# Seventeen of thirty modulation column blocks, weighted on VectorE and GpSimd and summed over rows by one matmul each, in place of eight matmul steps each

## The reference, cut to what matters

```python
silu_c = jax.nn.silu(c)            # (1, 1024), latents
silu_cc = jax.nn.silu(c_ctx)       # (1024,),  context
for l in range(DEPTH):             # DEPTH = 2
    m_lat = (silu_c @ w_mod[l] + b_mod[l]).reshape(Bsz, N_MOD, 1, D)    # N_MOD = 9
    m_ctx = (silu_cc @ w_mod[l] + b_mod[l]).reshape(N_MOD, D)
    x = x + 0.5 * m_lat[:, 2] * swiglu(modulate(rms_norm(x), m_lat[:, 0], m_lat[:, 1]), ...)
    ... mixer with m[3], m[4], m[5]; second feed-forward with m[6], m[7], m[8] ...
```

## Time and profile before

| | |
|---|---|
| runs | 3808.41 us median (3801.29 to 3816.84) |
| profiled execution, first to last instruction | 3809.4 us |
| TensorE busy | 3587.4 us, 94% |
| VectorE busy | 1836.3 us, 48% |
| ScalarE busy | 1418.9 us, 37% |
| GpSimd busy | 60.0 us, 2% |
| modulation matmuls | 960 records (two to a matmul, four matmuls to a step), 143.1 us |

### The profile page before, as it was taken

How to read it: one execution, slowest core, us unless ns; L and a number is a source line. 1 busy time by engine, 2 the same in 40 slices (tenths; PEclk the granted TensorE clock), 3 DMA queues, 4 the chain that set the end, 5 groups by cost and what they waited for, 6 DMA issues and landing times.

```text
span 3809.4 us, 62156 instructions
## 1 busy us (share of the span) xinstructions
PE 3587.4 (94%) x27294; PEld 2960.9 (78%) x27294; DVE 1836.3 (48%) x3143; ACT 1418.9 (37%) x2303; POOL 60.0 (2%) x98
## 2 busy tenths in 40 slices
PE   6999999888889999999987999999999989999898
PEld 4777885677668888877874998777887768879898
DVE  2223445666654233423265553654464443566575
ACT  3123334434334222323244543443243332445553
POOL 0000000000010000000000000020000000010000
PEclk8999999999999999999998999999999999999999
DMA  5454123222243233243225552121324552223463
GB/s 194 163 183 134 59 83 127 102 102 102 102 77 110 91 99 100 90 142 122 89 89 212 174 180 96 58 78 56 100 83 172 177 173 93 89 91 127 145 190 113
DMA packets 257918, 453.93 MB, mean 119 GB/s; under 512 B 14096, under 2 KB 157584, under 8 KB 243184
## 3 DMA queue, kind: packets, MB, share of 16 engines
q1 hardware_dynamic: 253840, 441.68, 34.6%
q0 software_dynamic: 3808, 8.27, 1.3%
HBM read 447.24 MB, written 1.94 MB: 118 GB/s over the span
## 4 chain that ended last, share of the span: by engine, by line
PE 81%; DVE 10%; ACT 4%; DMA 3%; issue 1%; SPq 0%; DVEq 0%; ACTq 0%
PE bank L1072 80%; DVE W L1859 2%; DVE W L1868 2%; DVE WR L1859 2%; DMA ring<-in_w_mod 1%; ACT WR L1524 1%; ACT W L1524 1%; PE bank L1295 1%; DMA ring<-in_w_up 1%; DVE H L1859 1%; DVE HL L1859 1%; DMA ring<-in_w_ada 1%; DVE X L1868 0%; ACT H L1524 0%; DVE small L2136 0%
## 5 line engine op out<-in xcount | busy, mean ns | idle before, releaser
L1072 PE MATMUL bank<-HH,WR 128*128 128x512 f32 (+1 forms) x9312 | 2430.9, 347 | 74.9 <-DVE WR L1859 42.0
L1072 PEld LDWEIGHTS bank<-HH,WR 128*128 128x128 f32 x9312 | 1643.3, 192 | 334.3 <-DVE WR L1859 54.4
L1072 PE MATMUL bank<-HL,WR 128*128 128x512 f32 (+1 forms) x4656 | 1601.3, 344 | 0.0
L1859 DVE TENSOR_TENSOR WR<-ring,WR 128x2048 fp32r<-128x2048 f32 (+3 forms) x300 | 673.8, 2250 | 859.9 <-ACT WR L1524 859.4
L1524 ACT ACTIVATE WR<-ring 128x2048 fp32r<-128x2048 f32 (+3 forms) x300 | 562.6, 1881 | 1200.1 <-PE bank L1072 819.5
L1072 PEld LDWEIGHTS bank<-HL,WR 128*128 128x128 f32 x4656 | 895.4, 192 | 96.9
L1524 ACT ACTIVATE W<-bank 64x256 f32<-64x256 f32 (+4 forms) x662 | 285.8, 442 | 388.6 <-PE bank L1072 342.1
L1072 PE MATMUL bank<-W 64*64 64x64 f32 (+5 forms) x6304 | 351.7, 247 | 41.4 <-ACT W L1524 20.5
L1072 PEld LDWEIGHTS bank<-W 64*64 64x64 f32 (+3 forms) x6304 | 266.1, 140 | 131.6 <-issue 47.2
L1868 DVE SCALAR_TENSOR_TENSOR W<-bank,vec,W 128x510 f32<-128x510 f32 (+1 forms) x206 | 130.6, 634 | 190.2 <-ACT W L1524 186.6
L1524 ACT ACTIVATE W<-bank,small 128x512 f32<-128x512 f32 (+2 forms) x183 | 113.1, 622 | 225.8 <-DVE small L2136 154.1
(11 more groups left out here) (111 smaller groups left out, 2022.0 us busy)
## 6 DMA issues: line engine op xcount, KB each, us to landing
ring<-in_ffn_in SPq DMA_DIRECT2D x176, 512.0 KB, 5.0
ring<-in_w_mod SPq DMA_DIRECT2D x72, 1024.0 KB, 5.4
ring<-in_w_in SPq DMA_DIRECT2D x52, 1024.0 KB, 5.1
ring<-in_w_ada SPq DMA_DIRECT2D x48, 1024.0 KB, 6.5
ring<-in_ffn_out SPq DMA_DIRECT2D x176, 256.0 KB, 3.6
ring<-in_w_up SPq DMA_DIRECT2D x88, 512.0 KB, 5.0
ring<-in_w_down SPq DMA_DIRECT2D x88, 256.0 KB, 3.6
ring<-in_even_w_in SPq DMA_DIRECT2D x8, 1024.0 KB, 5.1
```

Source lines behind the costliest of these rows:

```text
L1072: return e.matmul(o, l, r, start=start, stop=stop, skip_group_check=True)
L1859: put(e.tensor_tensor(o, a, b, op), *events)
```

## The change

Seventeen of the thirty blocks leave `mod_mm`: blocks 2 to 8 of `w_mod[0]`, 0 to 5 of `w_mod[1]`, 0 to 3 of `w_ada[0]`. For each, eight pieces of 128 rows by 1024 columns are loaded. VectorE multiplies a piece by the latents' value of each row and adds it to an accumulator; GpSimd does the same for the context in two instructions (product in place, then sum), except for one block of `w_mod[1]` that the context doesn't need. One TensorE step with ones then sums over the 128 rows (`rows_sum`), and four small matmuls turn the sums into columns (`rows_tr`), one such pair to a block.

All pieces stand in f00, 2 and f10: 40 behind the steps of the first product (a rate of 0.55 pieces to a step; in f10 8 of VectorE alone and 24 of both) and 8 behind the first steps of the second (rate 0.9). One ring slot is set aside for them in these stages, cut in two halves; weights have the other two. A piece's load is issued on GpSimd's queue when the piece two before it has been used by both engines. The silu of both vectors is made once at the start. The scan keeps 12 steps, the second attention 8.

```diff
+        ACC = [[wv(25088, [1024]), wv(27136, [1024])], [wv(9216, [1024]), wv(10240, [1024])]]
...
+        def row_sums(jobs, buf):
+            tail, ahead = [], []
+            for t, idx, nv in jobs:
+                for k in range(KD):
+                    s = rows_slab(TABLES[t][0], k, idx, nv)
+                    ORDER.append(("rows_in", s))
+                    ahead.append(("rows", t, idx, k, s, nv, buf))
+                    if len(ahead) > 1:
+                        ORDER.append(ahead.pop(0))
+                    if tail and k in (2, 4):
+                        ORDER.append(tail.pop(0))
+                    yield
+                now(ahead)
+                tail = [("rows_sum", t, idx, s, nv, buf), ("rows_tr", t, idx, nv)]
+                buf = 1 - buf
+            PENDING.extend(tail)
...
-        cols = {t: columns(t) for t in TABLES}
+        cols = {"m0": columns("m0", [0]), "m1": columns("m1", [3, 4]), "a0": columns("a0", [2]), "a1": columns("a1", [0, 1, 2])}
...
-        ffn("f00", A["ffn_in"][0, 0], A["ffn_out"][0, 0], 0, NT, 0, "ne", (itertools.islice(cols["m0"], 18), 0.85))
+        ffn("f00", A["ffn_in"][0, 0], A["ffn_out"][0, 0], 0, NT, 0, "ne",
+            rows=(row_sums(pairs_of("m0", 2, 7), 0), 0.55, row_sums(pairs_of("m0", 7, 8), 0), 0.9))
...
+            rows=(row_sums(pairs_of("m0", 8, 9) + pairs_of("m1", 0, 4), 0), 0.55, row_sums(pairs_of("m1", 4, 5), 0), 0.9))
-        ffn("f10", A["ffn_in"][1, 0], A["ffn_out"][1, 0], 0, NT, 1, "no", (itertools.islice(cols["a0"], 9), 0.5))
+        ffn("f10", A["ffn_in"][1, 0], A["ffn_out"][1, 0], 0, NT, 1, "no",
+            rows=(row_sums(pairs_of("m1", 5, 6, 1) + pairs_of("a0", 0, 3), 1), 0.55, row_sums(pairs_of("a0", 3, 4), 0), 0.9))
...
-                    if any(use[r] >= i for r in befores(todo[0], "raw")):
+                    if any(use[r] >= i for r in befores(todo[0], "raw", "rows")):
...
             def rows_sum(t, idx, s, nv, buf):                      # TensorE
+                q.wait_ge(DVES, ("rows", s))
+                if nv == 2:
+                    q.wait_ge(POOLS, ("rows", s))
+                for j in range(2):
+                    for v in range(nv):
+                        i = 32 * (nv * j + v)
+                        x = mm(o[i:i + 32, :], C("ones", 0, 32), ACC[buf][v][:, 512 * j:512 * j + 512], True, True)
...
+            def rows(t, idx, k, s, nv, buf):                       # VectorE
+                q.wait_ge(ROWS[SLABS[s]["half"]], ("raw", s))
+                c = SILU[src][:, k:k + 1]
+                if k == 0:
+                    ts(ACC[buf][0], rows_of(s), c, None, ALU.mult, None, ("rows", t, idx, k, 0), ("rows", s))
+                else:
+                    stt(ACC[buf][0], rows_of(s), c, ACC[buf][0], ALU.mult, ALU.add, ("rows", t, idx, k, 0), ("rows", s))
...
+            def rows_in(s):                                        # GpSimd
+                    q.wait_ge(POOLS, ("rows", x["before"])) if SLABS[x["before"]]["nv"] == 2 else q.wait_ge(DVES, ("rows", x["before"]))
+                e.dma_start(rows_of(s), x["parts"][0]).then_inc(ROWS[x["half"]].sem, ROWS[x["half"]].mark(("raw", s), by=16))
+            def rows(t, idx, k, s, nv, buf):                       # GpSimd
+                q.wait_ge(ROWS[SLABS[s]["half"]], ("raw", s))
+                q.wait_ge(DVES, ("rows", s))
+                if k == 0:
+                    e.tensor_scalar(ACC[buf][1], rows_of(s), c, None, ALU.mult).then_inc(...)
+                else:
+                    e.tensor_scalar(rows_of(s), rows_of(s), c, None, ALU.mult).then_inc(...)
+                    q.wait_ge(POOLS, ("rows_product", s))
+                    e.tensor_tensor(ACC[buf][1], ACC[buf][1], rows_of(s), ALU.add).then_inc(...)
```

More of the change, by code:

```diff
@@ L241, in program @@
         SLABS = []
-        hold = {"split": 0, "slots": 3, "slot": -1, "keep": None}
+        hold = {"split": 0, "slots": 3, "slot": -1, "keep": None, "halves": None}
         IN_SLOT = [None] * NS
@@ L268, in slab, with rows_begin, rows_end, rows_slab @@
             return IN_SLOT[i]
+        def rows_begin():
+            i = hold["keep"] = (hold["slot"] + 1) % NS
+            hold["halves"] = [IN_SLOT[i], IN_SLOT[i]]
+        def rows_end():
+            hold["slot"], hold["keep"], hold["halves"] = hold["keep"], None, None
+        def rows_slab(w, k, idx, nv):
+            i, h = hold["keep"], k % 2
+            SLABS.append(dict(parts=[w[P * k:P * k + P, 1024 * idx:1024 * idx + 1024]], kc=1, w=1024, kind="rows", half=h, nv=nv,
+                              split_from=hold["split"], slots=hold["slots"], ring=i, before=hold["halves"][h],
+                              n=sum(x["kind"] == "split" for x in SLABS)))
+            IN_SLOT[i] = hold["halves"][h] = len(SLABS) - 1
+            return IN_SLOT[i]
         def slot(s):
             return ring[SLABS[s]["ring"]]
+        def rows_of(s):
+            h = SLABS[s]["half"]
+            return slot(s).rearrange("p k c -> p (k c)")[:, 1024 * h:1024 * h + 1024]
         def landed(s):
@@ L314, in lin @@
                                     square(kw["norm"], 4 * g + m, h)
+                        if each:
+                            each()
                     if between:
@@ L1014, in program @@
                 use[step[6]] = i
+            if step[0] == "rows":
+                use[step[4]] = i
             if step[0] == "lora_done":
                 use[LORA["s"]] = i
-        befores = lambda s, kind: [x["before"] for x in SLABS[:s + 1] if x["before"] is not None and SLABS[x["before"]]["kind"] == kind]
+        befores = lambda s, *kinds: [x["before"] for x in SLABS[:s + 1] if x["before"] is not None and SLABS[x["before"]]["kind"] in kinds]
         steps, at_hold, behind_ = [], 0, []
         for i, step in enumerate(ORDER):
-            if step[0] in ("slab", "slab_h", "slab_k", "mod_mm"):
+            if step[0] in ("slab", "slab_h", "slab_k", "mod_mm", "rows"):
                 steps += [("rest", s) for s in behind_]
@@ L1026, in program @@
                 assert not todo or todo[0] not in befores(step[6], "split")
+            if step[0] == "rows":
+                assert not todo or todo[0] not in befores(step[4], "split")
             n = None
@@ L1057, in take @@
                 at[0] += 1
-                n = next(i for i, (t, b) in enumerate(shut_) if not (holder[b] and holder[b][0] == "bcast" and at[0] - t < 6))
+                n = next(i for i, (t, b) in enumerate(shut_) if not (holder[b] and holder[b][0] == "bcast" and at[0] - t < 8))
                 b = shut_.pop(n)[1]
@@ L1193, in mod_tr, with rows_sum, rows_tr @@
                            C("sel", 0, 2 * nb, 0, 32 * nb), True, True)
+                x.then_inc(MM.sem, MM.mark(key))
+                shut(key)
+            def rows_sum(t, idx, s, nv, buf):
+                key = ("rows", t, idx)
+                o = take(key)
+                q.wait_ge(IN["first"], ("in", "first"))
+                q.wait_ge(DVES, ("rows", s))
[5 more added lines that the diff above has]
+                        x = mm(o[i:i + 32, :], C("ones", 0, 32), ACC[buf][v][:, 512 * j:512 * j + 512], True, True)
+                x.then_inc(MM.sem, MM.mark(key))
+                shut(key)
+            def rows_tr(t, idx, nv):
+                key = ("rowsc", t, idx)
+                n = 2 * nv
+                q.wait_ge(ACTS, ("mrow", t, "rows", idx))
+                o = take(key)
+                for m in range(4):
+                    x = mm(o[:, n * m:n * m + n], RROW[0:32 * n, m * P:(m + 1) * P], C("sel", 0, 2 * n, 0, 32 * n)[:, ::2], True, True)
                 x.then_inc(MM.sem, MM.mark(key))
@@ L1512, in fourier_b @@
                 shut(("f2", l, n))
-            do = dict(slab=slab_, slab_h=slab_h, slab_k=slab_k, mod_mm=mod_mm, mod_tr=mod_tr, sum=sum_, rstd=rstd, spread=spread, spread_read=spread_read, bar=bar, rope=rope,
+            do = dict(slab=slab_, slab_h=slab_h, slab_k=slab_k, mod_mm=mod_mm, mod_tr=mod_tr, rows_sum=rows_sum, rows_tr=rows_tr, sum=sum_, rstd=rstd, spread=spread, spread_read=spread_read, bar=bar, rope=rope,
                       head_sum=head_sum, head_spread=head_spread, att=att, lora_w=lora_w, lora_a=lora_a, wkv=lambda d: next(streams[d]),
@@ L1535, in silu_c @@
                 src = TABLES[t][3]
[L1536 removed]
+                q.wait_ge(ACTS, ("silu", src))
                 q.wait_ge(DVES, ("silc_zero",))
@@ L2367, in nc_parts @@
                 tt(NCl[:, h, 0:nq], NCO[:, h, 0:nq], Sh[:, h, 0:nq].bitcast(F32), ALU.subtract, ("hl", f"sc{l}", h))
-            do = dict(begin=begin, inputs=inputs, inputs_rest=inputs_rest, rest=rest, mod_tr=mod_tr, rstd=rstd, times=times, mod_l=mod_l,
+            do = dict(begin=begin, inputs=inputs, inputs_rest=inputs_rest, rest=rest, mod_tr=mod_tr, rows=rows, rows_tr=rows_tr, rstd=rstd, times=times, mod_l=mod_l,
```

123 lines of the change are left out of this document (103 added, 20 removed).

## The result

| | before | after |
|---|---|---|
| runs, median | 3812.62 us (3801.29 to 3818.58, 4 runs) | 4047.41 us (4040.88 to 4057.56, 4 runs) |
| ratio | | 1.0623, 95% interval 1.0601 to 1.0645 |
| profiled span | 3809.4 us | 4046.5 us |
| mean granted clock | 0.974 | 0.946 |

Slower, as forecast, but by 235 us in the medians (237 between the two profiled executions) and not by 46: outside the range of 3778 to 3925. The rival nearest to it was the third (GpSimd is slow, 4002 us, given 0.09).

What follows compares the result with a forecast made beforehand. TensorE, with 81% of the chain of waits, was taken as the bound. Terms 7 - 48 + 47 (first products) + 32 + 8 = +46 on the profiled 3809.4 us gave 3855, 1 less against the median: 3854 us; range 3778 to 3925.

Steps and rivals of the forecast that it cites:

- the third rival: Feed-forwards: GpSimd slow, a piece every 6.4 us against 5.0 due even without exclusion; +194 us, 4002 us; chance 0.09.
- Elsewhere, forecast -48: Modulation steps leaving the scan (-24), first attention (-12, range -6 to -18) and second attention (-12): together -48 us.
- Own TensorE work, forecast +7: Feed-forwards: seventeen `rows_sum` and `rows_tr` add 36.0 us, the departing modulation work takes away 28.8: +7 us.
- GpSimd's pair, taken at 3.13 us: GpSimd's product and sum on a piece: three operand reads at ScalarE's 1.043 us, 3.13 us; ends 1.97 and 6.3.
- The forecast's own formula: Time per piece under exclusion: VectorE 1.21, GpSimd 2.87, low parts' share 1.04, hand-overs 0.2; 5.3 us against 5.0 due.
- The count of surplus times pieces: First products: 0.3 us over the due time per piece, times 40, 40 and 24 pieces: 12, 12 and 7 us.
- The fourth rival: Exclusion real and hand-overs worse, a piece at 6.0 us: another 60 us, 3914 us; counted inside the forecast's 0.47.
- Exclusion: VectorE instructions with two SBUF operands and GpSimd's exclude each other, so times add: a piece takes 5.3 us.
- the first rival: Side by side: VectorE and GpSimd don't exclude each other, GpSimd takes 3 to 4 us; +2 us, 3810 us; chance 0.27.
- Second products, forecast +32: Slab 1's low part waits behind five pieces; TensorE stands still 9.3 us, about 10.5 with exclusion, three times: +32 us.
- Nothing elsewhere: No other cost: two weight slots suffice, the pieces' bytes meet a low DMA share, the silu runs beside a load.
- Clock, forecast +8: TensorE at its lower clock after each of four long stalls, 1.9 us lost each time: +8 us.

Runs made afterwards that it cites:

- the seventh run: Changed kernel with the skew loads ahead of stage 2 and VectorE's piece instructions on 64 of 1024 columns, GpSimd whole, rate 0.9: 3954.01 us, ratio 1.0377.

## Why the prediction was wrong

**Where the time goes back to.** From the 3736.89 us without the blocks up to the 4047.41 of the change, in the order of the runs: 49 for the work itself on TensorE and VectorE (to 3786.13), 36 for the second products' rate (to 3821.99), 190 for GpSimd's arithmetic under that rate (to 4012.07), 35 for the `skew` loads. Parts interact, so the sizes hold for this order: the rate costs 36 with VectorE alone and 59 with GpSimd.

**Elsewhere, forecast -48: right.** -40.6; the scan's -26.1 within 2 us. The first attention gave 4.1 and not 12, below that term's low end. All 17.9 us of modulation matmuls are gone from it, but TensorE's busy time fell by 11.9 us only, at a granted clock of 0.94 in place of 0.97, and its idle time grew by 7.7.

**Own TensorE work, forecast +7: right in the count, a little small.** Spread and with VectorE alone, the feed-forwards are 16.4 us longer than before (3784.3 us of span, -41.5 us elsewhere, -25.1 in all), with some late low parts of the first products in it: the 512-column `HH,WR` matmuls wait 26.1 us for low parts, 15.0 before. The `rows_sum` steps were taken at no wait, two pieces behind their sums; in the change they hold TensorE twice for GpSimd's sum, 11.3 us together (6.39 in f00, 4.91 in 2).

**GpSimd's pair, taken at 3.13 us: the step that failed.** "I take the time of one operand read after the other at ScalarE's rate": it is 5.24 us. No row had an arithmetic instruction of GpSimd, the ends were 1.97 and 6.3, and the middle was taken because it was near a row, of another engine. The runs show it as the step: with GpSimd's instructions on 64 columns 180 us go, and with none of its arithmetic 190 (167 with the second products spread).

The forecast's own formula with 5.24 gives (7 x 5.24 + 2.85)/8 = 4.94 in place of 2.87, and a piece of 7.4 us in place of 5.3. The trace has 7.2 on average, but of other parts: 6.5 where no low part falls between, the wait for a load at each block's start, which the formula had not, and a longer product behind a low part. The count of surplus times pieces doesn't hold so well: 2.0 us over the 5.2 of VectorE alone, on 104 pieces, would be some 210 us, and the first products lost 157. What hid the rest is not shown.

The third rival had nearly that period, 6.4 us, from a pair too slow and no exclusion; its sum of 4002 stands 10 us from the 4012 measured once the `skew` loads are out of the way. In part that is luck: its pair was 1.0 us longer than the measured one, its issue and hand-overs 0.6 us shorter, and its second products took 75 where 57.7 were measured. It deserved more than 0.09: a due time of 5.0 us with a cost open from 2 to 6.3 is a coin toss on which side of the due time it falls.

Four sums of the prediction were off beside that. The ratio of 1.96 makes the sum instruction 0.3 us longer in seven of eight pieces, and over 104 pieces of surplus that adds 28 us and not 10, the way in which the miss went. The fourth rival's piece is 0.7 us longer, which makes 73 us and not 60, and so 3927, just outside the range that was said to hold it. The far end of the scan is some -40 and not -42, and the third rival's terms add to +195. None of them would have brought the forecast near 4047.

**Exclusion: right, but not what decided.** It was the forecast's mechanism, and it is there: 3.17 and 3.47 us where VectorE alone takes 1.28, 1.74 for an instruction of 0.27. The Trainium skill (SBUF — State Buffer, Who interferes with whom) has it that the shared pair of ports is an exclusive lock, that a VectorE instruction with two SBUF inputs contends with a GpSimd instruction that reads SBUF, and, for VectorE's two-port modes, that whoever issues first has the pair for the whole instruction and the other is fully blocked. The 1.08 us from the end of GpSimd's sum to VectorE's agree with a block of nearly a whole instruction: most of VectorE's own 1.28 us lies behind the other's end. Who came first can't be read off: VectorE's record starts 0.05 us before the sum's, and yet it was VectorE that waited. In the hand-over order of this kernel much of VectorE's wait lies beside GpSimd's own work, so it is not paid twice. How much of the loss is exclusion stays open: the seventh run gives 58 us for VectorE's piece instruction, length and exclusion together, and no run takes the low parts' exclusion away. Side by side at the measured lengths the first rival would have been slow too: 2.85 + 2.39 + 0.6 + 0.7 is over 5.0.

**Second products, forecast +32: mechanism right, size for the wrong kernel.** The low part of slab 1 does stand behind the pieces. Worked out at 9.3 us each, measured 9.79, 9.62 and 10.34 where VectorE does both vectors. In the change 18.17, 19.75 and 19.75, 57.7 in all, since each piece passes GpSimd at 6.5 us.

**"Nothing elsewhere": false.** I had looked at the pieces' loads for their own price and not for what stands in front of them on GpSimd's queue. The `skew` loads stand in stage 2's order between the pieces, 35 us. The trace of before had their 30 us on GpSimd's queue, and the prediction passed them by, since nothing waited behind them there.

**Clock, forecast +8: too small, as its stalls.** The mechanism holds: behind the 18.17 us of idle TensorE has a granted clock of 0.58.

```profile
415.16:419.16 4.00, 4.00 (x11) 3.20 (x12) 3.04 (x4) 0.00 (x0) 3.92 (x2) 0.58 0.76 242
```

All nine waits of over 7 us in the feed-forwards behind the start lead to such a stretch, with 0.50 to 0.58 over the next 4 us. The forecast had four. The 60 busy us more of the same matmuls are the size of it. They are inside the parts above, not beside them.

## What to carry to other kernels

If work is handed out at a fixed pace, what matters is on which side of the due time the slowest engine falls, with its issues and hand-overs counted; below it or near it little is paid (32 us for the first half of GpSimd's columns), above it much (147 for the second). Count the whole loop: where a buffer comes free only behind the slow engine, the load is a part of the pace. A cost open on both sides of that point calls for two cases of like weight, not for a middle value. Before a load is put on a queue, list what else is issued there in the same stretch, and on a strictly ordered engine put optional work behind what TensorE needs next, spread out: here that was worth 36 us, more than the 25 that the move gives in its best version.
